# Moving eight stationary tiles of a split-float32 matmul kernel to eight different byte positions modulo 512

## The reference

```python
# block 1: gated short convolution, SwiGLU, attention with a window of 128, SwiGLU
bcx = rmsnorm(h, g) @ w_in                       # 1024 x 3072
y = b_gate * causal_depthwise_conv3(c_gate * u, conv_w)
h = h + rmsnorm(y @ w_out, g2)
ff = (silu(g) * u) @ w_down                      # g, u = split(rmsnorm(h) @ w_gate_up)
...
# block 2: SwiGLU, latent attention beside retention, SwiGLU
h = h + 0.5 * swiglu_2(rms_norm(h, n1), w_gate, w_up, w_down)
proj = rms_norm(h, n2) @ w_in                    # split into the two mixers
h = h + concatenate([mla, retention]) @ w_o
h = h + 0.5 * swiglu_2(rms_norm(h, n3), w_gate, w_up, w_down)
```

## Time and profile before

| | |
|---|---|
| median of 3 runs | 1097.84 us (1095.18 to 1099.17) |
| the profiled execution | 1094.71 us, of which the span of instructions is 1092.7 |
| TensorE busy (PE) | 1068.0 us, 98% of the span |
| weight loads (PEld) | 875.0 us |
| VectorE (DVE), ScalarE (ACT), GpSimd (POOL) | 662.7, 554.2, 100.5 us |
| granted TensorE clock, mean | 0.996 of full speed |
| HBM read | 186.15 MB, 171 GB/s over the span |

### The profile page before, as it was taken

One profiled execution on the slowest core, in us unless ns is written; L12 is line 12 of the kernel. 1 busy time (PEld: TensorE's weight loads), 2 busy tenths in 40 slices (PEclk: granted clock), 3 DMA queues, 4 the chain that ended last, 5 costly groups with the idle time before them and its releaser, 6 DMA issues.

```text
span 1092.7 us, 14811 instructions
## 1 busy us (share of the span) xinstructions
PE 1068.0 (98%) x5038; PEld 875.0 (80%) x5038; DVE 662.7 (61%) x960; ACT 554.2 (51%) x887; POOL 100.5 (9%) x177
## 2 busy tenths in 40 slices
PE   9899999999997999999999999999999999999997
PEld 6798788888885678888887888888888888888886
DVE  5877745546687675546467554646668684645543
ACT  5644644445566564445455454545566633544442
POOL 1700100000010032000001000000118110000000
PEclk9999999999999999999999999999999999999999
DMA  7755446455653245455465545656454223556441
GB/s 262 276 189 179 154 159 220 166 186 194 208 178 112 63 169 177 165 197 191 158 222 179 191 164 184 197 165 217 156 208 154 78 100 132 191 158 220 162 154 39
DMA packets 52171, 187.80 MB, mean 172 GB/s; under 512 B 5968, under 2 KB 6112, under 8 KB 52128
## 3 DMA queue, kind: packets, MB, share of 16 engines
q1 hardware_dynamic: 50976, 184.05, 50.5%
q0 software_dynamic: 864, 3.07, 0.9%
q10 hardware_dynamic: 288, 0.11, 0.0%
HBM read 186.15 MB, written 1.05 MB: 171 GB/s over the span
## 4 chain that ended last, share of the span: by engine, by line
PE 89%; DVE 5%; DMA 2%; ACT 2%; issue 1%; POOL 0%; SPq 0%; DVEq 0%; POOLq 0%; ACTq 0%
PE pG L1458 16%; PE pG L1456 16%; PE pG L1457 16%; PE pD L1456 11%; PE pD L1458 11%; PE pD L1457 11%; PE pT L1461 3%; DVE w_low L1142 2%; DMA raw<-in_stream 2%; PE pG L1478 1%; PE pD L1461 1%; PE pT L1765 1%; PE pG L1752 1%; PE pG L1461 1%; PE pD L1726 1%
## 5 line engine op out<-in xcount | busy, mean ns | idle before, releaser
L1142 DVE TENSOR_TENSOR w_low<-raw,w_high 128x1024 fp32r<-128x1024 f32 x344 | 418.0, 1231 | 120.3 <-ACT w_high L891 110.4
L891 ACT ACTIVATE w_high<-raw 128x1024 fp32r<-128x1024 f32 x344 | 358.1, 1056 | 83.8 <-PE pG L1458 68.1
L1456 PE MATMUL pG<-w_high,xTh 128*128 128x512 f32 (+1 forms) x816 | 321.5, 394 | 2.6 <-DVE xTl L1176 1.6
L1458 PE MATMUL pG<-w_high,xTl 128*128 128x512 f32 (+1 forms) x816 | 313.7, 384 | 0.0
L1457 PE MATMUL pG<-w_low,xTh 128*128 128x512 f32 (+1 forms) x816 | 311.9, 382 | 0.0
L1456 PEld LDWEIGHTS pG<-w_high,xTh 128*128 128x128 f32 x816 | 153.5, 188 | 29.1 <-DVE xTl L1176 2.5
L1458 PEld LDWEIGHTS pG<-w_high,xTl 128*128 128x128 f32 x816 | 153.3, 188 | 28.9
L1457 PEld LDWEIGHTS pG<-w_low,xTh 128*128 128x128 f32 x816 | 153.8, 189 | 25.6
L1456 PE MATMUL pD<-w_high,aTh 128*128 128x512 f32 x384 | 153.3, 399 | 1.9 <-DVE aTl L1255 1.3
L1458 PE MATMUL pD<-w_high,aTl 128*128 128x512 f32 x384 | 151.9, 396 | 0.0
L1457 PE MATMUL pD<-w_low,aTh 128*128 128x512 f32 x384 | 151.9, 396 | 0.0
(11 more groups left out here) (235 smaller groups left out, 852.4 us busy)
## 6 DMA issues: line engine op xcount, KB each, us to landing
raw<-in_stream SPq DMA_DIRECT2D x344, 512.0 KB, 4.4
post<-in_posts POOLq DMA_DIRECT2D x5, 512.0 KB, 4.8
first_w<-in_stream SPq DMA_DIRECT2D x3, 512.0 KB, 6.2
out<-hg SPq DMA_DIRECT2D x4, 256.0 KB, 2.0
h<-in_x SPq DMA_DIRECT2D x2, 256.0 KB, 3.3
h<-in_x SPq DMA_DIRECT2D x1, 512.0 KB, 7.8
consts<-in_consts POOLq DMA_DIRECT2D x1, 416.0 KB, 4.5
consts<-in_consts ACTq DMA_DIRECT2D x1, 64.0 KB, 3.3
```

Source lines behind the costliest of these rows:

```text
L891: sc.activation(w_high[:, slot(static):slot(static) + CHUNK], raw[:, static % RAW * CHUNK:(static % RAW + 1) * CHUNK], ACT.Copy).then_inc( ...
L1142: ve.tensor_tensor(w_low[:, slot(static):slot(static) + CHUNK], raw[:, static % RAW * CHUNK:(static % RAW + 1) * CHUNK], w_high[:, slot(st ...
L1456: pe.matmul(dst, ah, hi, start=start, stop=False)
L1458: return pe.matmul(dst, al, hi, start=False, stop=stop)
```

## The change

Each of the eight tensors `xTh0`, `xTh1`, `xTl0`, `xTl1`, `aTh0`, `aTh1`, `aTl0`, `aTl1` gets a start address with a given residue relative to the end of `raw`, which is the start of `w_high`. `place_on` skips bytes until the address fits.

```diff
         raw = place("raw", [P, RAW * CHUNK], F32)
+        raw_end = at[0]
         w_high = place("w_high", [P, RING * CHUNK], F32R)
         w_low = place("w_low", [P, RING * CHUNK], F32R)
-        xTh = [place(f"xTh{t}", [P, KT, P], F32R) for t in range(2)]
-        xTl = [place(f"xTl{t}", [P, KT, P], F32R) for t in range(2)]
+        line = 512
+
+        def place_on(name, shape, dt, shift):
+            base = at[0] + (raw_end + shift - at[0]) % line
+            size = int(np.prod(shape[1:])) * 4
+            at[0] = (base + size + 31) // 32 * 32
+            return place(name, shape, dt, base)
+
+        xTh = [place_on(f"xTh{t}", [P, KT, P], F32R, (0, 64)[t]) for t in range(2)]
+        xTl = [place_on(f"xTl{t}", [P, KT, P], F32R, (128, 192)[t]) for t in range(2)]
+        at[0] = (at[0] + 63) // 64 * 64
...
-        aTh = [place(f"aTh{t}", [P, 2, P], F32R) for t in range(2)]
-        aTl = [place(f"aTl{t}", [P, 2, P], F32R) for t in range(2)]
+        aTh = [place_on(f"aTh{t}", [P, 2, P], F32R, (256, 320)[t]) for t in range(2)]
+        aTl = [place_on(f"aTl{t}", [P, 2, P], F32R, (384, 32)[t]) for t in range(2)]
+        at[0] = (at[0] + 63) // 64 * 64
...
-        rtmp = [place(f"rtmp{i}", [P, 12, ROT_HALF], F32) for i in range(4)]
+        rtmp = [place(f"rtmp{i}", [P, 12, ROT_HALF], F32, actT_at + 384 * i) for i in range(4)]
```

## The result

The changed kernel takes 1102.43 us (median of 5 runs, 1101.96 to 1103.77), the kernel before 1097.84 beside it. The ratio is 1.0043, with a 95% interval of 1.003 to 1.0056: slower by 4.6 us. The prediction said slower, by 8.5 us.

What follows compares the result with a forecast made beforehand. PE's own pass rate was taken as the bound nearly everywhere. Terms +8.0 + 2.0 + 0 - 1.5 + 0 gave +8.5 us, about 1106 us, with a range of 1090 to 1120 and the forecast's own range 1101 to 1112.

Steps and rivals of the forecast that it cites:

- The bound and the mechanism: PE's pass rate is the time; the next pass's weight load reads its tile while the present pass reads its weights.
- (a): `xT` passes moved off position 0: 1952 passes at 4.1 ns more each, +8.0 us.
- (b): 976 unmoved `xTh0` passes partly lose their settled 227 ns, as each third pass is `xTl0` at 128: +2.0 us.
- (c): `aT` passes, 960 of 1152 leaving 384, and `x2` and `latT` moved to 64: 0, bounds -16.2 and +7.0 us.
- (d): Slower passes partly hidden by PE's slack in the first stage and the kernel's remaining waits: -1.5 us.
- (e): Other edits, `rtmp` on the bytes of `aTh` and DVE writes of `aTl1` at a multiple of 32 bytes: 0.
- nothing happens: Rival: the two readers do not meet, block length explains the spacing; time 1097.8 us; chance 0.26, including a balance of prices.

Runs made afterwards that it cites:

- low_shifted: Changed kernel with `w_low`, `xTl`, `aTl` at 64 and `w_high`, `xTh`, `aTh` at 0: 1102.67 us, ratio 1.0046.
- all at 0: Changed kernel with all eight stationary tiles at position 0: 1089.03 us, ratio 0.9939.
- the restored positions: Changed kernel with `xT` tiles back at 0 and `aT` tiles at 384, rotation temporaries still on the bytes of `aTh`: 1098.27 us, ratio 1.0003.

## Why the prediction was right, and where it was off

**The bound and the mechanism** held, as far as the mechanism is that position sets the spacing. PE's passes are the time, the settling is lost when the `xT` tiles leave position 0, and no wait appeared. The picture behind it, a load that meets the pass beside it, was not shown, and in its simplest form it fell with `low_shifted`. The busy time of the 512-column `xT` groups into `pG` grew from 282.5 + 276.1 + 274.3 = 832.9 us to 282.6 + 278.6 + 277.3 = 838.5. With the groups into `pD`, 1.1 more, that is +6.7 us in the profiled executions.

**Terms (a) and (b)**, together +10.0 us, are the ones that were mis-sized: +6.7 in the groups, and +8.1 by the ratio of the run that moves these tiles alone. Per pass they come to 2.7 ns for t = 0 and 4.1 for t = 1; the blocks step by 230.5 and 231.4 ns, which is 1.9 and 2.8 more than 228.6. The price of 4.1 was the 232.7 of a whole `D` block, its first step from another kind of block included, less 228.6; from the second pass on 384 is at 232, 3.6 more. And it came from a uniform position, while in the change the `xT` tiles are in mixed pairs, 0 with 128 and 64 with 192. One neighbour stood for six positions, and they are not alike: 192 is at 229.1, 128 at 232.3, 64 at 233.2.

Step (b), that `xTh0` loses its settling although it did not move, is right: the `G` blocks of t = 0 average 230.5 and not the 228.6 that they had. Its premise, that settling takes some ten undisturbed passes, holds for the kernel before; with all at 0 it takes six. Whether the loss falls on `xTh0`'s passes or on `xTl0`'s can't be separated within a block, since one pass sets the phase of the next.

**Term (c)**, nothing for the `aT` tiles, was near: 457.1 us in the three groups before, 456.6 after, and -1.4 us by the ratio of its own run, whose interval reaches to zero. But it is a balance of two halves that the prediction did not have, and that they cancel is luck. The `D` blocks of t = 1 went from 232 to 235 ns a step, while over all `D` blocks the passes of the first line, to which the first pass of each block belongs, fell from 399 to 396 ns.

**Term (d)**, -1.5 us, was meant as slack that hides a cost. The cost was hardly there: the first line's passes of 384 columns went from 39.0 to 39.2 us. **Term (e)**: nothing for the temporaries is confirmed by the restored positions, 1.0003. Nothing for `aTl1` at a multiple of 32 bytes was not tested apart; VectorE has no more busy time than before.

The sum of +8.5 is thus too large mainly by (a): PE's busy time grew by 6.9 us in the profiled executions. The further step down to +4.6 lies in how the executions compared differ, the clock probably first. The measured 1102.43 us lies in the forecast's own range of 1101 to 1112, near its lower end, while +4.6 us is under the 5.5 at which the text had set "slower".

The rival "nothing happens" drew on the rule that TensorE never waits on another reader. The Trainium skill's page "SBUF — State Buffer", section "SBUF: two separate sides", gives weight loads a read port of their own. The runs here show that addresses modulo 256 bytes are worth 2 to 7.5 ns of a 227 ns pass all the same (192 and 96 in the table).

## What to carry to other kernels

When TensorE is the bound, read the starts of neighbouring passes, not their durations. If the same number of columns steps by different amounts in different places, compare the addresses of the operands before anything else. In a chain of `fp32r` passes, try all stationary tiles and all moving tiles at the same address modulo 256 bytes; here, with `w_high` at 128 modulo 256, that took 128 bytes of padding and was worth 0.9%. Whether another common address does as well was not run. And when a price is known at one address only, a kernel with several addresses, each in blocks of its own, gives several rows of the table in one trace.

## What the runs showed of the hardware that was not expected

- The period of the effect is 256 bytes: 0 and 256 step by 227 ns, 192 and 448 by 229, 96 and 352 by 234.
- The price is not a smooth function of the distance: 32 bytes off costs about as much as 128 (233.2 and 232.3 ns), and 192 off is the cheapest after 0 (229.1).
- It has a memory: the `D` block at 320 and 32 steps by 235 ns behind one kind of `G` block and by 231 behind another, and a `G` block at 0 settles after six passes behind a `D` block at 0 and after ten behind one at 384.
- A settled pass of 512 columns still takes 227 ns, 14 over the 213.3 of its columns, with all operands at one position. In no run did a block of such passes average less, and where the 14 ns come from stays open.
